# Four mixer layers on one core: norm sums by transposes, decay rows by DMA, and a new order of evacuations, loads and the forget gates

## What is computed

```
y = x * rsqrt(mean(x*x) + eps) * gain                 # rms norm: before each layer, on the SSD output,
                                                      # and on each head's attention output
log_f = log_sigmoid(f_f + f_b); c = cumsum(log_f)     # forget gates; c enters the logits of 8 heads
a_cs = cumsum(dt * A)                                 # SSD: one row of 512 per head, in chunks of 128
decay[l, s] = exp(a_cs[l] - a_cs[s]) for s <= l       # one matrix per head and chunk pair
o = rmsnorm(softmax_1 V - lam * softmax_2 V) * (1 - init) * silu(z)   # attention of layers 2 and 3
```

## Time and profile before

| | us |
|---|---|
| median of 3 runs | 3325.62 (3324.76 to 3325.98) |
| profiled execution, its own time | 3327.72 |
| its span | 3325.9 |
| busy in the span: PE | 3290.1 |
| DVE | 2080.6 |
| ACT | 1263.9 |
| POOL | 146.9 |

### The profile page before, as it was taken

How to read it: one execution, slowest core, us unless ns; L and a number is a source line. 1 busy time by engine, 2 the same in 40 slices (tenths; PEclk the granted TensorE clock), 3 DMA queues, 4 the chain that set the end, 5 groups by cost and what they waited for, 6 DMA issues and landing times.

```text
span 3325.9 us, 42719 instructions
## 1 busy us (share of the span) xinstructions
PE 3290.1 (99%) x15690; PEld 2677.0 (80%) x15690; DVE 2080.6 (63%) x3161; ACT 1263.9 (38%) x1987; POOL 146.9 (4%) x116
## 2 busy tenths in 40 slices
PE   8999999999999999999999999999999999999999
PEld 7888887787888888888888887787778888778777
DVE  5665656687765655534264786667756477666763
ACT  4333324445443344523142225424534223532541
POOL 3000000001020000000020000100002000000000
PEclk9999999999999999999999999999999999999999
DMA  5333435677776665746452443444547354345445
GB/s 177 128 121 105 138 127 186 222 243 267 254 261 207 192 204 179 244 171 209 151 186 99 156 159 130 153 134 165 200 160 252 107 173 148 131 142 169 169 164 203
DMA packets 297712, 580.88 MB, mean 175 GB/s; under 512 B 63768, under 2 KB 110616, under 8 KB 297504
## 3 DMA queue, kind: packets, MB, share of 16 engines
q1 hardware_dynamic: 297504, 578.16, 51.8%
HBM read 445.90 MB, written 132.14 MB: 174 GB/s over the span
## 4 chain that ended last, share of the span: by engine, by line
PE 82%; issue 12%; DVE 3%; DMA 1%; ACT 1%; POOLq 1%; DVEq 1%; SPq 0%; ACTq 0%
PE bank L560 62%; PE bank L559 10%; PE bank L2015 1%; PE bank L1596 1%; PE bank L1100 1%; POOLq L462 1%; PE bank L737 1%; PE bank L1421 1%; PE bank L1130 1%; PE bank L1452 1%; PE bank L1608 1%; DMA convert_in<-x 0%; PE bank L1610 0%; PE bank L1006 0%; DVE weights_low L472 0%
## 5 line engine op out<-in xcount | busy, mean ns | idle before, releaser
L560 PE MATMUL bank<-act_high,weights_high 128*128 128x512 f32 x3584 | 1426.6, 398 | 13.6 <-DVE act_low L543 11.3
L560 PE MATMUL bank<-act_low,weights_high 128*128 128x512 f32 x3584 | 1403.4, 392 | 0.0
L472 DVE TENSOR_TENSOR weights_low<-weights_raw,weights_high 128x1024 fp32r<-128x1024 f32 x528 | 654.4, 1240 | 752.3 <-ACT weights_high L403 740.7
L403 ACT ACTIVATE weights_high<-weights_raw 128x1024 fp32r<-128x1024 f32 x528 | 558.5, 1058 | 1443.8 <-PE bank L560 1200.5
L560 PE MATMUL bank<-act_high,weights_low 128*128 128x512 f32 x3584 | 963.3, 390 | 0.0
L560 PEld LDWEIGHTS bank<-act_high,weights_high 128*128 128x128 f32 x3584 | 676.4, 189 | 164.7 <-DVE act_low L543 11.3
L560 PEld LDWEIGHTS bank<-act_low,weights_high 128*128 128x128 f32 x3584 | 677.2, 189 | 135.7 <-issue 1.2
L560 PEld LDWEIGHTS bank<-act_high,weights_low 128*128 128x128 f32 x3584 | 673.1, 188 | 139.6
L559 PE MATMUL bank<-weights_high,act_high 128*128 128x512 f32 x640 | 253.9, 397 | 3.9 <-DVE stream_out L501 3.1
L559 PE MATMUL bank<-weights_high,act_low 128*128 128x512 f32 x640 | 249.8, 390 | 0.0
L2113 DVE SCALAR_TENSOR_TENSOR residual_in<-residual_in,arena 128x512 f32<-128x512 f32 x240 | 182.1, 759 | 20.9 <-issue 2.4
(11 more groups left out here) (325 smaller groups left out, 2576.5 us busy)
## 6 DMA issues: line engine op xcount, KB each, us to landing
weights_raw<-in_w_all SPq DMA_DIRECT2D x528, 512.0 KB, 3.6
convert_in<-mix SPq DMA_DIRECT2D x80, 256.0 KB, 4.5
fm_b<-stream_out SPq DMA_DIRECT2D x72, 256.0 KB, 2.6
mix<-arena SPq DMA_DIRECT2D x64, 256.0 KB, 3.2
x_part<-stream_out SPq DMA_DIRECT2D x48, 256.0 KB, 4.5
residual_in<-x_part SPq DMA_DIRECT2D x48, 256.0 KB, 5.5
x<-stream_out SPq DMA_DIRECT2D x48, 256.0 KB, 5.4
convert_in<-x SPq DMA_DIRECT2D x48, 256.0 KB, 4.2
```

Of the source, the lines that this page charges most:

```text
L403: e.activation(WH[:, t % 3, :], RAW[:, t % 3, :], ACT.Copy).then_inc(wh_ready, 1)
L472: e.tensor_tensor(WL[:, t % 3, :], RAW[:, t % 3, :], WH[:, t % 3, :].bitcast(F32), ALU.subtract).then_inc(wl_ready, 1)
L560: return e.matmul(bank[s][:, :], a[:, s * P:(s + 1) * P], h, start=start, stop=stop)
```

## The change

Sums of the norms and their spreads are made by transposes; the sum over the channels is then a reduction along the columns on DVE. The decay rows come from DRAM by a broadcast DMA per head. DVE evacuates four pass ends per layer (slots 47, 55, 63, 71) before the low part, in iteration t itself, with only the convolution taps behind it; and in slots 5 and 6 of each attention head its stage steps stand before the low part. The forget gates are worked out in slots 12 to 15, and head 0's loads are issued at slot 77, q and k first. The statistic of layer 3 is one slot later. The first attention head takes its gate from the buffer in which the pass was evacuated (OUTB). SP issues the conversions' loads before the weights, and stores pass 32 last in its iteration.

```diff
-STAT = {0: 5, 2: 148, 5: 276, 7: B[0] + 132}
+STAT = {0: 5, 2: 148, 5: 276, 7: B[0] + 133}
...
@@ stat_pe: sums, then spreads
-                    mm = e.matmul(mid[3][:, a * TB + b:a * TB + b + 1], (ACC2 if a else ACC[:, :])[:, b * P:(b + 1) * P],
-                                  ONES[:, 0:1], start=True, stop=True)
+                    mm = e.transpose(mid[3 - a][:, b * P:(b + 1) * P], (ACC2 if a else ACC[:, :])[:, b * P:(b + 1) * P],
+                                     IDENT[:, :])
...
-                    mm = e.matmul(mid[3 - a][:, b * P:(b + 1) * P], SQ[:, a, b * P:(b + 1) * P], IDENT[:, :],
-                                  start=True, stop=True)
+                    mm = e.transpose(mid[3 - a][:, b * P:(b + 1) * P], SQ[:, a, b * P:(b + 1) * P], IDENT[:, :])
@@ stat_dve
-            e.tensor_scalar(NM[:, 0, :], mid[3][:, 0:TB], 1.0 / width, EPS, ALU.mult, ALU.add).then_inc(*st_d.mark("mean"))
+            for a in range(2 if two else 1):
+                e.tensor_reduce(NM[:, a, :], mid[3 - a][:, :].rearrange("p (b n) -> p b n", b=TB), AX, ALU.add)
+            e.drain()
+            e.tensor_scalar(NM[:, 0, :], NM[:, 0, :], 1.0 / width, EPS, ALU.mult, ALU.add).then_inc(*st_d.mark("mean"))
...
@@ gla_sp, before the load of the masks
+                e.wait_ge(fx_cst, 16)
@@ forget_sp, forget_dve: the waits for GLA_DONE go; forget_pe:
-            for x in GLA_DONE:
-                e.wait_ge(*x)
+            e.wait_ge(*sm_d.at("out"))
@@ fox_sp
+        def fox_load(e, h):
+            stored(e, 11 if h >= 4 else 7)
+            e.dma_start(fx_q, FMD[0][16 + h]).then_inc(fx_in, 16)
+            e.dma_start(fx_k, FMD[0][24 + h]).then_inc(fx_in, 16)
+            for b in range(TB):
+                e.dma_start(rows(fx_r, b), FCR[h:h + 1, 0:(b + 1) * P].broadcast_to([P, (b + 1) * P])).then_inc(fx_rin, 16)
+
+        def fox_first_sp(e):
+            for x in GLA_DONE:
+                e.wait_ge(*x)
+            fox_load(e, 0)
             yield
 
         def fox_sp(e, h):
             if h:
                 e.wait_ge(*fx_p.at("lc", h - 1))
                 e.wait_ge(*fx_d.at("m1", h - 1))
-            else:
-                for x in GLA_DONE:
-                    e.wait_ge(*x)
-                e.wait_ge(fx_cst, 16)
-            for b in range(TB):
-                e.dma_start(rows(fx_r, b), FCR[h:h + 1, 0:(b + 1) * P].broadcast_to([P, (b + 1) * P])).then_inc(fx_rin, 16)
-            stored(e, 11 if h >= 4 else 7)
-            e.dma_start(fx_q, FMD[0][16 + h]).then_inc(fx_in, 16)
-            e.dma_start(fx_k, FMD[0][24 + h]).then_inc(fx_in, 16)
+                fox_load(e, h)
@@ ssd_pre: one more step (six slots)
+            e.wait_ge(*sd_td.at("rows", l))
+            e.dma_start(AD[l], sd_acs[0:16, 0, :]).then_inc(sd_ast, 16)
...
-            e.activation(SMW[:, :, :], sd_pick.rearrange("p (h o) -> p h o", o=1).broadcast_to([P, 16, P]), ACT.Copy
-                         ).then_inc(*sd_ta.mark("pick"))
...
-            e.tensor_copy(ROWS_R[:, :], mid[1][:, :])
-            e.drain()
-            low = slice(64, P)
-            e.tensor_tensor(ROWS_R[low, :], mid[1][low, :], ROWS_R[low, :].bitcast(F32), ALU.subtract)
-            e.drain().then_inc(*sd_td.mark("rows"))
+            e.tensor_copy(sd_acs[0:16, 0, :], mid[1][0:16, :]).then_inc(*sd_td.mark("rows"))
@@ ssd_sp
+            if h >= 2:
+                e.wait_ge(*sd_afar.at("far", t - 2))
+            else:
+                e.wait_ge(sd_ast, 16 * (l + 1))
+            e.dma_start(sd_acs[:, h % 2, :], AD[l][h:h + 1, :].broadcast_to([P, L])).then_inc(sd_ain[h % 2], 16)
@@ ssd_pe
-            e.matmul(mid[h % 2][:, :], SMW[:, h, :], ROWS_R[:, :], start=True, stop=True).then_inc(*sd_pacs.mark("acs"))
@@ ssd_dve; in ssd_act too the rows are read from sd_acs
-            e.wait_ge(*sd_pacs.at("acs", t))
-            ee, ps = sd_e[h % 4], mid[h % 2]
+            e.wait_ge(sd_ain[h % 2], 16 * (l * 8 + h // 2 + 1))
+            ee, ps = sd_e[h % 4], sd_acs[:, h % 2, :]
@@ att_sp
-            stored(e, B_FIRST[l] + 11)
-            e.dma_start(at_z, FMB[l][32 + h]).then_inc(at_zin, 16)
+            if h:
+                stored(e, B_FIRST[l] + 11)
+                e.dma_start(at_z, FMB[l][32 + h]).then_inc(at_zin, 16)
@@ att_pe: the sum by four transposes of at_sq into mid[1]; att_dve:
-            e.tensor_scalar(at_st, mid[1][:, 0:TB], 1.0 / P, EPS, m, add).then_inc(*d.mark("mean"))
+            e.tensor_reduce(at_st, mid[1][:, :].rearrange("p (b n) -> p b n", b=TB), AX, add)
+            e.drain()
+            e.tensor_scalar(at_st, at_st, 1.0 / P, EPS, m, add).then_inc(*d.mark("mean"))
...
-            e.wait_ge(at_zin, 16 * (l * 4 + h + 1))
-            e.scalar_tensor_tensor(at_sq, mid[1][:, :], at_li[:, 1:2], at_z, m, m)
+            if h:
+                e.wait_ge(at_zin, 16 * (l * 3 + h))
+            else:
+                e.wait_ge(*DONE[B_FIRST[l] + 11, 0])
+            e.scalar_tensor_tensor(at_sq, mid[1][:, :], at_li[:, 1:2], at_z if h else OUTB[:, 0, :], m, m)
@@ the plan of the slots
-        stage("forget", place(75, 4), sp=forget_sp, pe=forget_pe, act=forget_act, dve=forget_dve)
+        stage("forget", place(12, 4), sp=forget_sp, pe=forget_pe, act=forget_act, dve=forget_dve)
+        stage("fox_first", place(77, 1), sp=fox_first_sp)
...
-        STAGE_FIRST = {*range(16, 24), *(B[l] + t for l in range(2) for t in range(17, 72))}
+        STAGE_FIRST = {*range(16, 24), *(B[l] + t for l in range(2) for t in range(17, 72)),
+                       *(B[l] + ATT_START[h] + i for l in range(2) for h in range(4) for i in (5, 6))}
...
+        EVAC_MID = {t for t, q in ENDS.items() if t in STAGE_FIRST and t in feeds_pe and q not in RF_FIRST}
@@ SP's loop
-                if t - 1 in ENDS:
+                late = t - 1 in ENDS and LAYER[ENDS[t - 1]] >= 2 and PASSES[ENDS[t - 1]].index == 32
+                if t - 1 in ENDS and not late:
                     store_sp(e, ENDS[t - 1])
                 take(t)
+                for n in LOAD_AT.get(t, ()):
+                    convert_sp(e, n)
                 if t + 5 < NU:
                     weights_sp(e, t + 5)
...
-                for n in LOAD_AT.get(t, ()):
-                    convert_sp(e, n)
+                if late:
+                    store_sp(e, ENDS[t - 1])
@@ DVE's loop
-                if t - 1 in ENDS and t - 1 not in EVAC_SOON:
+                if t - 1 in ENDS and t - 1 not in EVAC_SOON | EVAC_MID:
                     evac_dve(e, ENDS[t - 1])
-                if t in STAGE_FIRST and t not in EVAC_SOON:
+                if t in EVAC_MID:
+                    take(t, conv=False)
+                    evac_dve(e, ENDS[t])
+                    take(t, rest=False)
+                elif t in STAGE_FIRST and t not in EVAC_SOON:
                     take(t)
                 if t + AHEAD < NU:
                     weights_dve(e, t + AHEAD)
```

More of the change, by code:

```diff
@@ L220, in build @@
         SMO = sb("small_out", [P, L])
-        ROWS_R = sb("rows_rounded", [P, L], F32R)
         ONES = sb("ones", [P, P])
@@ L227, in build @@
         GLUB = sb("glu_bias", [P, KT])
-        ARENA_N = 19520
+        ARENA_N = 20032
         ARENA = sb("arena", [P, ARENA_N])
@@ L1374, in forget_dve @@
             yield
+        def fox_load(e, h):
[8 more added lines that the diff above has]
+            fox_load(e, 0)
+            yield
         def fox_sp(e, h):
@@ L1711, in build @@
         sd_mx = [sem(f"sd_mix{n}") for n in range(2)]
-        sd_tp, sd_ta, sd_td = steps("sd_dt_pe", "dt sums"), steps("sd_dt_act", "ln pick"), steps("sd_dt_dve", "pad y a tot rows")
+        sd_tp, sd_ta, sd_td = steps("sd_dt_pe", "dt sums"), steps("sd_dt_act", "ln"), steps("sd_dt_dve", "pad y a tot rows")
         sd_cp, sd_ca, sd_cd = steps("sd_conv_pe", "xt"), steps("sd_conv_act", "silu"), steps("sd_conv_dve", "conv")
@@ L1715, in build @@
         sd_gp, sd_ga, sd_gd = steps("sd_cb_pe", "cb"), steps("sd_cb_act", "far"), steps("sd_cb_dve", "near")
-        sd_pacs, sd_py = steps("sd_pe_acs", "acs"), steps("sd_pe_y", "y")
+        sd_py = steps("sd_pe_y", "y")
         sd_afar = steps("sd_act_far", "far")
@@ L1720, in build @@
         XD = [dram(f"ssd_x{l}", [8, P, L]) for l in range(2)]
+        AD = [dram(f"ssd_acs{l}", [16, L]) for l in range(2)]
+        sd_ast, sd_ain = sem("sd_acs_stored"), [sem(f"sd_acs_in{n}") for n in range(2)]
         A = Arena(0, B_END)
@@ L1731, in build @@
         sd_w, sd_dsk, sd_pick = A(12, 5), A(8), A(16)
+        sd_acs = A(2, L)
         after_conv = Arena(0, 6 * L)
@@ L1996, in ssd_pe @@
             t, k = l * 16 + h, h // 2
-            if h >= 2:
-                e.wait_ge(*sd_afar.at("far", t - 2))
-            else:
-                e.wait_ge(*sd_ta.at("pick", l))
-                e.wait_ge(*sd_td.at("rows", l))
-                e.wait_ge(*sd_ga.at("far", l * 2 + 1))
-                e.wait_ge(*sd_gd.at("near", l * 2 + 1))
```

(11 more changed lines are left out.)

17 lines of the change are left out of this document (6 added, 11 removed).

## The result

The changed kernel takes **3305.3 us** (median of four runs, 3302.1 to 3307.9); the kernel before takes 3325.8 beside it. The ratio is 0.9933, with a 95% interval of 0.992 to 0.9945: faster, by 20.5 us and not by 35.5, and outside the predicted range. Run again beside its variants, it took 3302.3 us (3300.1 to 3304.8), a ratio of 0.9926 [0.9914, 0.9938].

A forecast was written before the change was run, and what follows sets the result against it. PE's order of work bounds the kernel: 2872 us of units fixed, some 450 movable. Gains less 1.3 of new waits sum to 35.5 us, taking 3327.7 to 3292.2; the median, 2.1 lower, is 3290.1, range 3282 to 3302.

The forecast's parts named there:

- cost zero: Decay-row broadcasts: landings up to 9.5 us (7.2 in the first four heads) cost nothing on DVE.
- Sums and spreads by transposes: Statistics and attention heads: 22 groups at 0.45 us give 9.9, less 1.3 for new waits behind DVE's reductions.
- Decay rows by DMA: Attention heads, two layers: 32 matmuls of 0.23 us leave PE, a gain of 7.4 us.
- first sign of failure: In the changed profile, DVE waits for the acs rows would show the forecast wrong; no size given.
- the rival with late rows: Rival 2, chance 0.04: late broadcasts slow the 16 two-head loops; landings of 13 us would give 3346 us.
- Evacuations ahead of low parts: Pass ends in the state-space part, two layers: PE's waits for late evacuations go, 7.6 us, between 0 and 8.2.
- Attention turns: Head 0's slots: stage work before the low part saves 3.2 of the 4.0 us PE waits for softmax weights.
- Forget gates: Work moved to slot 12 with room on DVE and ACT, cost 0; earlier loads at slot 80 gain 4.6 us.
- Load order elsewhere: Loads one issue of weights earlier: 0.5 us gained around the split output passes' ends, between -2 and 2.
- The statistic of layer 3 and head 0's mix: Statistic one slot later ends PE's wait for POOL, 0.8 us; head 0's mix no longer late, 2.8 us.
- The base: Whole kernel: the median of the runs was put 2.1 us below the profiled execution's 3292.2, giving 3290.1.
- Rival 1: Chance 0.17: PE's waits return in another form since DVE's order is full; 3302.2 us.

The follow-up runs named there:

- c2: Changed kernel with the norms' and heads' sums and spreads by plain matmuls again and no reduction on DVE: 3310.3 us, ratio 0.9944.
- b3: Kernel before with only the sums and spreads by transposes and the reductions on DVE: 3326.42 us in eleven runs, ratio 1.0.
- b2: Changed kernel with the decay rows by the matmul of one-hot picks again, all else as changed: 3302.99 us, ratio 0.9926.
- c3: Kernel before with only the evacuations of slots 47, 55, 63 and 71 of layers 2 and 3 ahead of the low parts: 3319.46 us, ratio 0.9969.
- a2: Changed kernel with the conversions' loads again behind the weights in SP's iteration: 3299.99 us, ratio 0.9922.
- the control: The changed kernel once more, as it is, run beside its variants: 3302.29 us (3300.12 to 3304.82).
- c1: Changed kernel with SP issuing two heads' decay rows ahead of the stores at the passes' ends: 3295.52 us, ratio 0.99.

## Why the prediction missed

The step that failed is the "cost zero" of the decay rows: 8.4 us in slots 335, 336, 463 and 464, part of it at half clock. The other pieces of the miss are side effects that the sum put at nothing or too low (the loads 2.9, the forget gates 2.4) and the clock.

- **Sums and spreads by transposes** (8.6): right. 0.47 per group in the chain, the reduction 0.69 us, the new waits where they were named, 0.5 us and twice 0.2 for 0.7 and twice 0.3; c2 measures 8.0. It holds only with the other parts: alone it gives nothing (b3).
- **Decay rows by DMA** (7.4): "cost zero" was wrong. The gain on PE is there, 0.13 to 0.35 in each slot. The cost was argued from the landing, and rightly (up to 5.7 us in the first four heads, where the limit was 7.2, and up to 7.5 later, where it was 9.5). What I left out is when SP can issue the row: I listed what stands behind it in the queue and not what stands before it, the stores of the pass, which wait for ACT. The same reasoning had found this very thing for head 0's mix. In place of 7.4 the rows brought 0.7 (b2), with 7 us back once they were issued in time (c1). The forecast did name DVE waits for the acs rows as its first sign of failure; the rival with late rows was priced as a loop of landings, not as two queue positions per layer.
- **Evacuations ahead of low parts** (7.6): right by itself, 8.6 in c3's slots. In the changed kernel slots 335 and 463 went the other way, through the rows.
- **Attention turns** (3.2): the slots 361 to 366 and 489 to 494 gained 3.4 and 2.0 us, more than forecast, but not by the mechanism alone, since the clock moved with it.
- **Forget gates** (0 at the new place): wrong by 2.4 us. "DVE and ACT follow PE with room" overlooked that the step holds each of the two engines for 5 us, and the high and low parts and the evacuation of a pass stand behind it. The 4.6 at slot 80 came in full (slots 76 to 80: 36.37 to 30.59, 5.8 with the moved matmul).
- **Load order elsewhere** (0.5, between -2 and 2): -2.9 at slots 271/272, beyond its bound; a2 got 2.3 of it back. An earlier load starts POOL's adds earlier, and they ran beside DVE's passes, which took longer.
- **The statistic of layer 3 and head 0's mix** (0.8 and 2.8): right (slots 404 to 406 take 2.1 less, 0.9 of it the transposes'; slots 370 and 498 1.27 and 1.60 less).
- **The base.** I took the profiled run's distance to the median, 2.1 us, as fixed. It is a matter of a few half-clock stretches more or less, which each run of this kernel draws anew: 5.3 us of the miss. How far such draws go the same kernel shows: its two medians are 3305.3 and 3302.3.

Rival 1, the waits come back in another form, gave 3302.2, and the control's 3302.3 hits it by luck: of its mechanism only the late evacuations came, and they came through the rows' place in SP's queue, not for want of room on DVE.

## What to carry to other kernels

When a value moves from an engine to a DMA, look at what stands ahead of it in the queue, with the waits of those entries, before looking at its landing. When a step is moved, add up how long it holds each engine in one piece and ask what is due there in that slot. Measure parts both alone and taken out: here the transposes were worth 0 alone and 8 in company, and the rows 0.7 until two issues changed places.

## What the hardware showed beyond that

- DVE passes that read SBUF often take longer when an add of POOL runs beside them. In the profile of after, 14 of the 24 low parts beside an add took 2.28 to 2.32 us and the other ten 1.21 to 1.23, as the low parts alone do; the pass of 0.75 us took up to 1.86, the add 1.28 to 2.40. I saw it in every trace and did not test it by itself, and why ten escaped is open.
- The move of the rows has a price here that the forecast lacks. In before the near passes read the row from a PSUM bank, and 44 of them that ran beside POOL took 0.34 to 0.35 us, like all others. In after they read it from SBUF: 0.27 to 0.29 alone, but 0.53 to 1.24 in the 12 that ran beside POOL. In c1 this cost PE nothing that can be seen.
- In thirteen of the fourteen profiles stretches at 1.2 GHz, 3.41 or 6.83 us long, stand mostly around the same waits of PE (slots 194, 271, 335, 361, 463, 489), but not in every run: after the same wait of 3.15 us behind unit 271 some profiles have no such stretch, some one of 3.41 and some one of 6.83 us.
